# One 512-column matmul for both token parts where the weights stand, and VectorE to add the two sums

## The reference, cut to what matters

```
k = (m @ wk)          # 256 memory tokens x 1024 -> 1024, both layers
q = (h @ wq)          # 256 tokens x 1024 -> 1024, both layers
(silu(h @ wg) * (h @ wu)) @ wd     # layer 0 only, D_FF = 2816
```

## Time and profile before

| | |
|---|---|
| median of 3 runs | 1628.78 us (1627.68 to 1636.58) |
| profiled execution | 1629.6 us span, from its first to its last instruction; no separate time of that execution is given |
| mean granted TensorE clock | 0.997 of full speed |
| TensorE matmuls | 8686, busy 98% of the span |
| VectorE, ScalarE busy | 75%, 63% |

### The profile page before, as it was taken

The page is one execution under the profiler, slowest core; times in us unless marked ns, Lnnn a source line. Parts: engine busy times, 40 slices in busy tenths (PEclk is TensorE's granted clock), DMA queues, the critical chain, the costliest instruction groups (busy, mean ns, idle before and its releaser), DMA issues.

```text
span 1629.6 us, 22097 instructions
## 1 busy us (share of the span) xinstructions
PE 1597.7 (98%) x8686; PEld 1358.2 (83%) x8686; DVE 1228.8 (75%) x1110; ACT 1022.3 (63%) x993; POOL 75.0 (5%) x61
## 2 busy tenths in 40 slices
PE   7999999999999999999999999999999999999997
PEld 6779889999787998888888878888888888888886
DVE  5755455444666655989898898898899889889886
ACT  6644443333555444677777677777777777777774
POOL 1000000000000001000000010010000010010010
PEclk9999999999999999999999999999999999999999
DMA  8524335555443445799999999999999999999993
GB/s 328 208 82 178 130 125 197 180 189 195 162 169 137 161 155 219 273 384 404 363 382 383 362 382 376 376 378 378 386 382 382 370 386 375 362 392 379 374 380 134
DMA packets 39164, 470.83 MB, mean 289 GB/s; under 512 B 4416, under 2 KB 4672, under 8 KB 9408
## 3 DMA queue, kind: packets, MB, share of 16 engines
q1 hardware_dynamic: 35136, 455.00, 72.4%
q0 software_dynamic: 3824, 14.49, 2.9%
q10 hardware_dynamic: 144, 0.52, 0.1%
HBM read 463.18 MB, written 6.82 MB: 288 GB/s over the span
## 4 chain that ended last, share of the span: by engine, by line
PE 71%; DMA 12%; DVE 9%; ACT 3%; issue 3%; SPq 0%; POOLq 0%; DVEq 0%; POOL 0%; ACTq 0%
PE PS L831 22%; PE PS L833 21%; PE PS L832 21%; DMA stage<-wm_dram 10%; DVE wlo L1893 5%; ACT whi L710 2%; DVE wlo L1416 1%; DMA stage<-wl_dram 1%; PE PS L1319 1%; DMA w1v<-wl_dram 1%; PE PS L1154 1%; PE PS L1134 1%; PE PS L903 1%; ACT whi L428 1%; DVE e_lo L1906 0%
## 5 line engine op out<-in xcount | busy, mean ns | idle before, releaser
L1893 DVE TENSOR_TENSOR wlo<-stage,whi 128x2048 fp32r<-128x2048 f32 x330 | 740.2, 2286 | 104.2 <-ACT whi L710 103.5
L710 ACT ACTIVATE whi<-stage 128x2048 fp32r<-128x2048 f32 x328 | 610.6, 1911 | 221.8 <-DMA stage<-wm_dram 214.0
L831 PE MATMUL PS<-whi,e_hi 128*128 128x512 f32 x896 | 355.3, 397 | 0.0
L833 PE MATMUL PS<-whi,e_lo 128*128 128x512 f32 x896 | 349.7, 390 | 0.0
L832 PE MATMUL PS<-wlo,e_hi 128*128 128x512 f32 x896 | 348.6, 389 | 0.0
L1416 DVE TENSOR_TENSOR wlo<-stage,whi 128x2048 fp32r<-128x2048 f32 (+2 forms) x62 | 200.9, 3242 | 139.7 <-ACT whi L428 139.7
L428 ACT ACTIVATE whi<-stage 128x2048 fp32r<-128x2048 f32 (+2 forms) x64 | 172.8, 2702 | 117.7 <-PE PS L833 104.6
L833 PEld LDWEIGHTS PS<-whi,e_lo 128*128 128x128 f32 x896 | 168.1, 188 | 36.3
L832 PEld LDWEIGHTS PS<-wlo,e_hi 128*128 128x128 f32 x896 | 168.5, 188 | 33.3
L831 PEld LDWEIGHTS PS<-whi,e_hi 128*128 128x128 f32 x896 | 168.3, 188 | 33.0 <-issue 0.3
L831 PE MATMUL PS<-whi,a_hi 128*128 128x512 f32 x448 | 175.6, 392 | 3.1 <-DVE a_lo L1981 3.0
(11 more groups left out here) (334 smaller groups left out, 1946.5 us busy)
## 6 DMA issues: line engine op xcount, KB each, us to landing
stage<-wm_dram SPq DMA_DIRECT2D x168, 2048.0 KB, 9.9
stage<-wl_dram SPq DMA_DIRECT2D x20, 2048.0 KB, 7.7
stage<-wf_dram SPq DMA_DIRECT2D x33, 1024.0 KB, 4.8
stage<-wl_dram SPq DMA_DIRECT2D x7, 1816.0 KB, 9.1
w1k<-wl_dram SPq DMA_DIRECT2D x2, 2048.0 KB, 8.6
w1v<-wl_dram SPq DMA_DIRECT2D x2, 2048.0 KB, 7.7
xs<-mem_dram POOLq DMA_DIRECT2D x2, 1024.0 KB, 8.2
stage<-wl_dram SPq DMA_DIRECT2D x4, 454.0 KB, 7.2
```

The source lines that it names most:

```text
L710: nc.scalar.activation(whi[kind][:, half], stage[kind][:, half], ACT.Copy).then_inc(w_hi[kind] if part else half_hi[kind], 1)
L831: mm(out, ah, bh, start=start, stop=False)
L833: return mm(out, al, bh, start=False, stop=stop)
L1893: ins = V.tensor_tensor(wlo[kind][:, half], stage[kind][:, half], f32(whi[kind][:, half]), ALU.subtract)
```

## The change

Where weights stand and tokens move, the three matmuls of a product become two. The two parts of the tokens lie one behind the other (`pairA`, `pairB`); the weights' high part meets both in one matmul of 2 x 256 columns, which fills a whole PSUM bank; the weights' low part then meets the high token part and adds into the bank's first half. VectorE reads both halves and adds them with a reduction over the pair, two banks at a time.

So a group n now has a bank of its own. `by_feature` uses banks 4 to 7 in every call, VectorE alone takes the results out, twice in each call, and call i waits for the banks of call i-1. In the dense mixer VectorE adds the pair into `f_sil` ahead of the silu, which then reads and writes `f_sil` in SBUF, and into `f_act` ahead of the product. VectorE's sum for `up(0)` stands ahead of its weight splitting in each step. Three semaphores are merged or renamed, and `keep_busy` writes bank 0, with a wait for the last silu.

```diff
-        hiA, loA = at("hiA", 16 * K, ...), at("loA", 24 * K, ...)   (hiB, loB likewise)
+        pairA, pairB = at("pairA", 16 * K, [2, KD, SEQ], F32R), at("pairB", 32 * K, [2, KD, SEQ], F32R)
+        hiA, loA, hiB, loB = pairA[:, 0], pairA[:, 1], pairB[:, 0], pairB[:, 1]
...
# ScalarE
-                kvq(0)
                 hi_layer(l, 8)
                 norm_hi(l, 1, "g_x", hiB)
-                kvq(1)
-                hi_layer(l, 9)
-                kvq(2)
-                hi_layer(l, 10)
-                kvq(3)
-                hi_layer(l, 11)
+                for s in range(9, 12):
+                    hi_layer(l, s)
...
-                        if first:
-                            act.wait_ge(w_used[2], 1)
-                        else:
-                            act.wait_ge(w_used[0], t)
-                            act.wait_ge(f_mul, t + 0)
-                        nc.scalar.activation(f_sil[:], bank(0), ACT.Silu).then_inc(f_silu, 1)
+                        act.wait_ge(f_sum, t * 2 + 1)
+                        nc.scalar.activation(f_sil[:], f_sil[:], ACT.Silu).then_inc(f_silu, 1)
...
# TensorE
+                def pair_product(out, wh, wl, pair, k):
+                    mm(out, wh, pair[:, :, k, :], start=(k == 0), stop=False, skip_group_check=True)
+                    return mm(out[:, 0, :], wl, pair[:, 0, k, :], start=False, stop=(k == KD - 1), skip_group_check=True)
...
-                    if i >= 2:
-                        pe.wait_ge(kvq_act, l * 6 + (i - 1))
-                        pe.wait_ge(kvq_dve, l * 6 + (i - 1))
                     for n in range(4):
+                        if i and n % 2 == 0:
+                            pe.wait_ge(kvq_dve, l * 10 + (2 * (i - 1) + n // 2 + 1))
...
-                        out = bank(4 + 2 * (i % 2) + n // 2)[:, (n % 2) * 256:(n % 2) * 256 + 256]
+                        out = bank(4 + n).rearrange("p (a n) -> p a n", a=2)
                         for k in range(KD):
                             cols = slice(n * P, (n + 1) * P)
-                            ins = product(out, wh[:, k, cols], wl[:, k, cols], ah[:, k, :], al[:, k, :], k == 0, k == KD - 1)
+                            ins = pair_product(out, wh[:, k, cols], wl[:, k, cols], pair, k)
...
# TensorE, in up
-                                ins = product(bank(kind)[:, n * 256:(n + 1) * 256], ..., hiB[:, k, :], loB[:, k, :], ...)
+                                ins = pair_product(bank(2 * kind + n).rearrange("p (a n) -> p a n", a=2), ..., pairB, k)
...
-                    keep_busy(2, 18)
+                    pe.wait_ge(f_silu, FF_STEPS)
+                    keep_busy(0, 18)
...
# VectorE
+            def both_parts(b):
+                return PS[:, b:b + 2, :].rearrange("p b (a n) -> p b n a", a=2)
...
                 def kvq(i):
+                    if i < 4:
+                        for b in range(2):
+                            dve.wait_ge(kvq_done, l * 12 + (2 * i + b + 1))
+                            c = 4 * (i % 2) + 2 * b
+                            V.tensor_reduce((kx_T, q_x_T)[i // 2][:, c:c + 2, :], both_parts(4 + 2 * b), AX, ALU.add).then_inc(kvq_dve, 1)
...
                     def dense(t, first=False, last=False):
+                        if first:
+                            dve.wait_ge(w_used[2], 1)
+                        else:
+                            dve.wait_ge(w_used[0], t)
+                        V.tensor_reduce(f_sil[:].rearrange("p (c t) -> p c t", c=2), both_parts(0), AX, ALU.add).then_inc(f_sum, 1)
                         if not last:
                             flo(0, t + 1)
                         else:
                             lo(0, PER_LAYER[0] + 1, KD * ZW)
                         flo(2, t)
+                        dve.wait_ge(w_used[1], t + 1)
+                        V.tensor_reduce(f_act[:].rearrange("p (c t) -> p c t", c=2), both_parts(2), AX, ALU.add).then_inc(f_sum, 1)
                         dve.wait_ge(f_silu, t + 1)
-                        dve.wait_ge(w_used[1], t + 1)
-                        V.tensor_tensor(f_act[:], f_sil[:], bank(1), ALU.mult).then_inc(f_mul, 1)
+                        dve.wait_ge(f_sum, t * 2 + 2)
+                        V.tensor_tensor(f_act[:], f_sil[:], f_act[:], ALU.mult).then_inc(f_mul, 1)
```

More of the change, by code:

```diff
@@ L589, in _ @@
                 squares(x, l * NT)
-                dests = [kx_T[:, 0:2, :], kx_T[:, 4:6, :], q_x_T[:, 0:2, :], q_x_T[:, 4:6, :], v_x[:, 0, 0:512], v_x[:, 0, 512:1024]]
                 def kvq(i):
                     act.wait_ge(kvq_done, l * 12 + (2 * i + 1))
-                    src = bank(4 + 2 * (i % 2))
-                    src = src if i >= 4 else src.rearrange("p (c t) -> p c t", c=2)
-                    nc.scalar.activation(dests[i], src, ACT.Copy).then_inc(kvq_act, 1)
-                kvq(0)
+                    nc.scalar.activation(v_x[:, 0, (i - 4) * 512:(i - 3) * 512], bank(4 + 2 * (i % 2)), ACT.Copy).then_inc(kvq_act, 1)
                 hi_layer(l, 8)
                 norm_hi(l, 1, "g_x", hiB)
-                kvq(1)
-                hi_layer(l, 9)
-                kvq(2)
-                hi_layer(l, 10)
-                kvq(3)
-                hi_layer(l, 11)
+                for s in range(9, 12):
+                    hi_layer(l, s)
                 kvq(4)
@@ L1090, in _, with by_feature @@
                     out_part(1, t, range(KD), start=True, stop=True)
-                def by_feature(i, s, ah, al):
+                def pair_product(out, wh, wl, pair, k):
+                    mm(out, wh, pair[:, :, k, :], start=(k == 0), stop=False, skip_group_check=True)
+                    return mm(out[:, 0, :], wl, pair[:, 0, k, :], start=False, stop=(k == KD - 1), skip_group_check=True)
+                def by_feature(i, s, pair):
                     pe.wait_ge(w_lo[s % 2], l * PER_LAYER[s % 2] + (s // 2 + 1))
@@ L1103, in by_feature @@
                         for k in range(KD):
                             cols = slice(n * P, (n + 1) * P)
-                            ins = product(out, wh[:, k, cols], wl[:, k, cols], ah[:, k, :], al[:, k, :], k == 0, k == KD - 1)
+                            ins = pair_product(out, wh[:, k, cols], wl[:, k, cols], pair, k)
                         if n % 2:
                             ins.then_inc(kvq_done, 1)
-                by_feature(0, 6, hiA, loA)
-                by_feature(1, 7, hiA, loA)
+                by_feature(0, 6, pairA)
@@ L1111, in _ @@
+                by_feature(1, 7, pairA)
                 pe.wait_ge(n_lo, l * 8 + 8)
-                by_feature(2, 8, hiB, loB)
-                by_feature(3, 9, hiB, loB)
+                by_feature(2, 8, pairB)
+                by_feature(3, 9, pairB)
                 def values(hf, t):
-                    s, i = 10 + hf, 4 + hf
+                    s = 10 + hf
                     if t == 0:
                         pe.wait_ge(w_lo[hf], l * PER_LAYER[hf] + (s // 2 + 1))
-                        pe.wait_ge(kvq_act, l * 6 + (i - 1))
-                        pe.wait_ge(kvq_dve, l * 6 + (i - 1))
+                        pe.wait_ge(kvq_dve, l * 10 + (7 + hf))
@@ L1127, in _ @@
                 values(0, 0)
-                pe.wait_ge(kvq_act, l * 6 + 4)
-                pe.wait_ge(kvq_dve, l * 6 + 4)
+                pe.wait_ge(kvq_dve, l * 10 + 8)
                 for t in range(NT):
@@ L1149, in _ @@
                     if h % 2 == 0:
-                        pe.wait_ge(kvq_act, l * 6 + (h // 2 + 5))
-                        pe.wait_ge(kvq_dve, l * 6 + (h // 2 + 5))
+                        pe.wait_ge(kvq_act, l * 2 + (h // 2 + 1))
+                        pe.wait_ge(kvq_dve, l * 10 + (h // 2 + 9))
                     for dc in range(2):
@@ L1205, in up @@
                                 cols = slice(n * P, (n + 1) * P)
-                                ins = product(bank(kind)[:, n * 256:(n + 1) * 256], wh[:, k, cols], wl[:, k, cols], hiB[:, k, :], loB[:, k, :],
-                                              k == 0, k == KD - 1)
+                                ins = pair_product(bank(2 * kind + n).rearrange("p (a n) -> p a n", a=2), wh[:, k, cols], wl[:, k, cols], pairB, k)
                         ins.then_inc(w_used[slot], 1)
@@ L1629, in _ @@
                 unit_max(l, 2, 0, 0)
-                dve.wait_ge(cmp_e, l + 1)
+                dve.wait_ge(small_e, l * 2 + 2)
                 V.tensor_reduce(cmax, lc, AX, ALU.add).then_inc(cmp_v, 1)
@@ L1671, in _ @@
                 norm_scale(x, l * 2 + 2)
-                dests = [kx_T[:, 2:4, :], kx_T[:, 6:8, :], q_x_T[:, 2:4, :], q_x_T[:, 6:8, :], v_x[:, 1, 0:512], v_x[:, 1, 512:1024]]
                 def kvq(i):
[L1675 to L1678, removed]
+                    if i < 4:
[4 more added lines that the diff above has]
+                    else:
+                        dve.wait_ge(kvq_done, l * 12 + (2 * i + 2))
+                        V.tensor_copy(v_x[:, 1, (i - 4) * 512:(i - 3) * 512], bank(5 + 2 * (i % 2))).then_inc(kvq_dve, 1)
```

(10 more changed lines are left out.)

14 lines of the change are left out of this document (6 added, 8 removed).

## The result

The kernel with the change takes 1638.68 us, the median of 6 runs (1635.14 to 1643.44). The kernel before, timed beside it, takes 1631.58 us (6 runs, the three above among them, 1627.68 to 1636.58). The ratio is 1.0046, with a 95% interval of 1.0032 to 1.006: slower by about 7 us (the medians differ by 7.1, the interval says 5.2 to 9.8). The prediction said +5.4 us and 1634.2 (1630 to 1639). Of the 4.5 us between 1634.2 and 1638.68, 2.8 are there because the median of the kernel before is 1631.58 with all six runs and was 1628.78 with three; the change itself cost 1.7 us more than forecast, and +5.4 lies inside the interval. The measured middle lies within the half per cent to which it gave 0.80, near the upper edge, and the interval reaches past that edge.

The account below looks back on a forecast made before the run. TensorE, busy 98% of the span, was taken as the bound through its matmul spacing and waits. Cross-attention +4.4, dense mixer -2.4 and clock falls +3.4 made +5.4 us, carried to the 1628.8 median: 1634.2, range 1630 to 1639.

Parts of the forecast that it names:

- the half per cent to which it gave 0.80: Whole kernel: time stays within 0.5% (8.1 us) of the kernel before, chance 0.80; slower 0.18, faster 0.02.
- The stall: Cross-attention, both layers: call 1 waits for VectorE's first sum of call 0; TensorE idle 3.9 us, call 1 3.46 late.
- Nothing was late after it: Cross-attention: after call 1's wait, VectorE's later sums come in time, so calls 1 to 3 each save 0.43 us.
- The sums take 1.22 us: VectorE's reductions of 1024 PSUM elements take 1.22 us each, with upper bound 1.76.
- rival 2: VectorE's sums of pairs take 1.76 us each: +2.7 us, 1633.5 without a fall, 1636.9 with two; chance 0.10.
- Stall less the returns of calls 1 to 3: Cross-attention: +3.46 us late less 3 x 0.43 = 1.28 saved, +2.2 us a layer, +4.4 for two.
- The tail: Dense mixer's end: last `up(1)`'s sum adds 1.22 us to the reload's chain, later ScalarE 0.4; together +1.6 us.
- VectorE never held up a `down(t)`: Dense mixer's steps: the 3.7 us chain feeding `down(t)` is hidden behind 5.55 us of `up(0, t+1)`; uncovered, 1.3 a step.
- Two falls behind three stalls: Granted clock after idle stretches in both layers and before the last `down`: two falls of 1.7 us each, +3.4 us.
- so each `up` gives its 0.21: Dense mixer: products fall from 0.360 to 0.347 us, each `up` saves 0.21; 19 `up`s give -4.0 us.
- Rival 1: Pair products save nothing, alternating widths keeping 0.24 behind each 256: +8.5 us, 1637.3 without a fall, 1640.7 with two; chance 0.12.
- dense mixer: Dense mixer as a whole: -4.0 us from the `up`s and +1.6 at its end, sum -2.4 us.

Follow-up runs that it names:

- the kernel with the early sums: Against the changed kernel, VectorE's first sum of call 0 moved ahead of the norm's scaling, the second staying behind it; median 1631.16 us, ratio 1.0001.
- one with a last step of its own: Changed kernel plus call 0's first sum before the norm, step 10's `up`s as before without sums, 22 small matmuls before the last `down`; 1628.78 us, ratio 0.9974.

## Why the prediction came out as it did

**What held.** The stall: its place, its releaser, its price (call 1 late by 3.37 for 3.46 forecast; 3.43 us idle for 3.9) and its cause. Moving the first sum, and nothing else, removes it. Nothing was late after it: calls 2 and 3 start without a wait. The sums take 1.22 us, so rival 2 (1.76) falls. Stall less the returns of calls 1 to 3 was +2.2 a layer; with the clock kept it measured 2.31 and 2.34, so +4.65 for +4.4. The tail was +1.6 and measured +1.69, by the route foretold: the first sum and the silu pushed ScalarE's split of slot 0 back. VectorE never held up a `down(t)`. Two falls behind three stalls were forecast; in the profiled execution two came, though not by an even chance each. Behind the 3.4 us stalls of layer 0 and 1 the clock fell in this kernel and in the one with `by_feature` alone, four times of four; behind the 2.59 us wait ahead of the last `down` it kept up here and fell in the kernel with the early sums. The fall in the routing, worth 0.8 us between the two profiled executions, was in no term.

**The step that failed** is "so each `up` gives its 0.21", the saving of a product in the dense mixer. I took 0.347 us a product because nearly the whole of a stream at either width showed the same fixed part of 0.0133. That holds in calls 2 and 3 and in the first 48 products of the mixer. The other 256 run at 0.3533: half of the fixed part comes back. So 19 `up`s return 48 x 0.0134 + 256 x 0.0067 = 2.4 us instead of 4.0. From the first product to the end of `down(8)` the trace shows 2.1 (158.65 before, 156.54 after), as a matmul of a `down` also takes about 0.0015 us more. With the tail the mixer gives 0.42 instead of 2.4. That is 2.0 us that the forecast counted as gained and that never came. My two bounds for the saving, nothing and 0.0146, did hold the 0.0067; I put no weight on the middle. Rival 1 named the right term, but not its size. The saving of 6.7 ns is measured; why the products take 0.3533 and not 0.3467 us stays open.

**A smaller miss.** I priced a fall at 1.7 us, from a stretch full of work. Here two cost 1.31 and 1.44, 2.8 instead of 3.4. The difference between the kernels with and without small matmuls measures it. That a fall can cost less than its share of TensorE's time shows at the earlier trace rows too: from the turning of the tokens to call 0 of layer 1 five traces with a fall took 111.3 to 112.9 us (the kernel before 111.93), and seven without one 111.0 to 111.6.

**The sum** by its own terms: cross-attention 4.65 for 4.4, clock 2.8 for 3.4, dense mixer -0.4 for -2.4, together +7.0 for +5.4, and the medians show +7.1. The time lies inside the range by 0.3 us only, and the upper end was put there for rival 1. That it lies inside is partly luck: two errors, 2.0 and -0.6, in part cancelled. What I held too firmly was 0.80 for "within 0.5%": +5.4 with terms open by 2 us each lies nearer to the bound of 8.1 than that chance says. The measured interval lies wholly above 1: a slowdown, and not the change too small to tell that the prediction held likeliest.

The Trainium skill, "TensorE: Matmul & The Clock Gate", section "Wait — 56ns, not 53.3ns?", gives a warm matmul N/2.4 GHz plus about 2.5 ns. By that, as an estimate, a removed one returns 2.5 ns. The runs show 13.4 ns returned in calls 2 and 3 and 6.7 in the dense mixer: the sign agrees, and the figure is too low in both.

## What to carry to other kernels

Here each matmul saved at equal columns returned 7 to 13 ns, so 608 of them were never worth more than 8 us, and one late wait of 3.4 us in each of two layers ate that and more. Where an edit gives up double buffering between calls, look first at where the copy that frees the banks stands in its engine's order: put it at the moment the bank is full, and fill the idle time that is left ahead of dense work with small matmuls, since a fall of the clock cost 1.3 to 1.4 us on top of the 2.3 that a stall cost. With both, the same change is 0.28% faster than the kernel before (0.15 to 0.42%; 0.2% by the medians), where as written it is 0.46% slower. And when marks of single executions are added up, look at the granted clock of the unedited stretches too: one of them alone was up to 2.5 us off here.

## What the runs showed of the hardware

**Two levels of spacing.** A product of a 512-column and a 256-column matmul, each with its own weights, starts every 0.3465 or every 0.3533 us at the same full clock, and keeps to its level over a whole run of 32 or 48. The same code in the same place is at one level in one trace and at the other in another: the first 48 of the mixer are quick with the early sums and slow when 22 small matmuls more stand at its end, over 180 us later. One trace of each doesn't tell whether the kernel or the execution decides it.

**The clock.** Waits of 3.4 us inside dense work were followed by 0.50 of the full clock each of four times; waits of 2.59 us were followed by a fall in some kernels and not in others. 30 small matmuls in the stall, or 40 ahead of the last `down`, kept it at 1.00. Work of many small matmuls can lose it as well: the routing of layer 1, unedited, ran at full clock in the kernel before (12.60 us) and in part at 0.50 in the kernel with the change (13.43) and with the early sums (15.07).

**Equal transfers.** The same load of the next weights at the end of the mixer took 8.96 us in the kernel before and 10.31 in one with a last step of its own, and these 1.35 us were nearly as much as the 1.7 that the sums cost in the tail.
